# A late u row's fetch is queued two v rows earlier in the dense experts stage

## The reference, cut to what matters

```python
idx = jnp.take_along_axis(cand_i, best_p, axis=-1)       # 128 experts of 16384 for each token
gate = jax.nn.softmax(best_s, axis=-1)
act = jnp.einsum('td,thkd->thk', xb, u_tab[ib])          # x . u of each chosen expert
wgt = jax.nn.gelu(act) * gb
y = jnp.einsum('thk,thkd->td', wgt, v_tab[ib])           # weighted sum of the v rows
```

## Time and profile before

| | us |
|---|---|
| median of three runs | 3286.01 |
| the profiled execution, its own time | 3282.5 |
| its span | 3280.7 |
| PE busy | 3122.7 (95%) |
| DVE busy | 2381.6 (73%) |
| ACT busy | 1406.0 (43%) |
| POOL busy | 641.9 (20%) |

### The profile page before, as it was taken

The page is one execution under the profiler, slowest core; times in us unless marked ns, Lnnn a source line. Parts: engine busy times, 40 slices in busy tenths (PEclk is TensorE's granted clock), DMA queues, the critical chain, the costliest instruction groups (busy, mean ns, idle before and its releaser), DMA issues. The chain is left out here.

```text
span 3280.7 us, 52721 instructions
## 1 busy us (share of the span) xinstructions
PE 3122.7 (95%) x17744; PEld 2695.4 (82%) x17744; DVE 2381.6 (73%) x4997; ACT 1406.0 (43%) x2735; POOL 641.9 (20%) x556
## 2 busy tenths in 40 slices
PE   7899999999999999899989999999999989999999
PEld 5757776777768899888976988988879977988888
DVE  6567776876656686556977777877656788877887
ACT  5454333333346565565264333332564274333332
POOL 0000000000000000155262222222356061222221
PEclk9899999999999999899999999999999999999999
DMA  6115533445323555433518899998334518998996
GB/s 218 42 58 180 173 141 122 141 129 166 95 67 109 159 168 172 142 113 129 176 43 290 316 331 336 334 336 327 129 101 155 167 70 301 338 332 312 338 341 246
DMA packets 176404, 643.35 MB, mean 196 GB/s; under 512 B 20352, under 2 KB 20736, under 8 KB 175360
## 3 DMA queue, kind: packets, MB, share of 16 engines
q1 hardware_dynamic: 138672, 504.62, 45.2%
q0 software_dynamic: 36864, 134.23, 11.4%
q10 hardware_dynamic: 720, 2.71, 0.2%
HBM read 640.44 MB, written 1.05 MB: 196 GB/s over the span
## 5 line engine op out<-in xcount | busy, mean ns | idle before, releaser
L338 ACT ACTIVATE split<-ring 128x512 fp32r<-128x512 f32 (+1 forms) x644 | 397.7, 624 | 699.3 <-PE ps L224 666.7
L224 PE MATMUL ps<-hT,split 128*128 128x512 f32 (+1 forms) x3504 | 630.5, 341 | 6.5 <-DVEq L322 3.5
L224 PEld LDWEIGHTS ps<-hT,split 128*128 128x128 f32 x3504 | 546.1, 191 | 91.1 <-DVE hT L593 9.7
L2696 PE MATMUL ps<-h2F,gates 128*128 128x192 f32 x3200 | 557.5, 328 | 18.1 <-DMA gates<-peer_u 17.9
L2696 PEld LDWEIGHTS ps<-h2F,gates 128*128 128x128 f32 x3200 | 530.9, 191 | 43.9 <-DMA gates<-peer_u 15.2
L347 POOL TENSOR_TENSOR split<-ring,split 128x512 fp32r<-128x512 f32 x184 | 244.6, 1340 | 1529.4 <-ACT split L338 1524.9
L347 DVE TENSOR_TENSOR split<-ring,split 128x512 fp32r<-128x512 f32 (+1 forms) x460 | 307.5, 679 | 283.8 <-ACT split L338 282.9
L2762 ACT ACTIVATE split<-ring 128x512 fp32r<-128x512 f32 x504 | 317.5, 632 | 348.4 <-PE ps L2713 316.2
L2686 POOL DMA_INDIRECT gates<-peer_rows,row_at x256 | 277.0, 1082 | 855.4 <-DVE row_act L2828 471.9
L2821 DVE TENSOR_TENSOR split<-ring,split 128x512 fp32r<-128x512 f32 x504 | 342.7, 691 | 125.5 <-ACT split L2762 125.3
L2755 ACT ACTIVATE gelu<-ps 128x192 f32<-128x192 f32 x200 | 66.2, 331 | 421.3 <-PE ps L2696 421.3
(11 more groups left out here) (389 smaller groups left out, 4753.0 us busy)
## 6 DMA issues: line engine op xcount, KB each, us to landing
ring<-peer_v SPq DMA_DIRECT2D x256, 512.0 KB, 5.6
gates<-peer_u SPq DMA_DIRECT2D x200, 512.0 KB, 6.6
ring<-w_up SPq DMA_DIRECT2D x88, 512.0 KB, 3.7
ring<-w_choose SPq DMA_DIRECT2D x88, 512.0 KB, 3.4
ring<-w_mixing SPq DMA_DIRECT2D x68, 512.0 KB, 3.5
ring<-w_merge SPq DMA_DIRECT2D x64, 512.0 KB, 4.2
ring<-w_down SPq DMA_DIRECT2D x44, 512.0 KB, 3.6
mix_row_ring<-w_mod SPq DMA_DIRECT2D x40, 512.0 KB, 3.7
```

The source lines that it names most:

```text
L224: ins = nc.tensor.matmul(out, lhsT(a), rhs(b), start=first and n == 0, stop=last and n == len(PASSES) - 1)
L338: self.nc.scalar.activation(self.split[:, self.half_slot(s), 0, cols], self.ring[:, self.slot(s), cols], ACT.Copy).then_inc(self.high_read ...
L2696: last = nc.tensor.matmul(k.ps[:, m % 2, 0:DENSE], k.u_ring[:, m % RAW, c * P:(c + 1) * P], k.h2F[:, c, 0:DENSE], start=c == 0, stop=c == ...
```

## The change

u row j - 28 now stands behind v row j, from j = 32 on, and no u row is left for behind the loop. What `fetch_u` waits for, the slots, the number of fetches and all work of the other engines stay as they were.

```diff
                 weights.fetch(sp, j // RAW, j % RAW)
                 if j in first_u:
                     fetch_u(first_u[j])
-                if j - EARLY - 2 >= RAW:
-                    fetch_u(j - EARLY - 2)
-            for q in range(rows - 2, rows):
-                fetch_u(q)
+                if j - EARLY >= RAW:
+                    fetch_u(j - EARLY)
             if ahead:
                 ahead.begin(sp, weights)
```

## The result

The changed kernel took 3266.78 us in the median of 13 runs (3248.15 to 3275.31), the kernel before 3293.03 us in 13 runs (3278.22 to 3310.24). The ratio is 0.9918 with a 95% interval of 0.9896 to 0.9941: 26 us, 0.8% faster. The forecast was 27.1 us less 1, and a time of 3258. The median of before was itself 7 us higher in 13 runs than in the three shown first.

The account below looks back on a forecast made before the run. PE was taken to bound the kernel, losing time only to late u rows: 3282.5 - 27.1 for waits + 1 for transfers = 3256.4 us, or 3259.9 from the median; predicted 3258, with 8 in 10 for 3248 to 3276.

Parts of the forecast that it names:

- What bounds the kernel: Whole kernel: PE, busy 95% of the span, bounds it; in the late part it waits only for u landings.
- What the waits cost in all: Both layers, first to last activate: excess over the clean beat of 12.97 + 14.16 = 27.1 us, all expected to go.
- The 5.8 us of restarts and short waits: Late part: slower restarts after waits and waits too short to list, about 0.36 us for each of 16, expected to go.
- The 3.5 us for activates at the lower clock: Late part: two activates after long waits run partly at the lower clock, some 1.75 us each, expected to go.
- Why u is late: Late u fetches: lead of 7.6 to 7.9 us against landings up to 9.8; an extra dot product delays the issue.
- The new wait in SP's queue: SP, steady part: the wait for u's slot ends before the next v row could be issued, 4 us to spare; cost nothing.
- At the turn: Start of each late part: v row 33 goes out 1.5 us late behind u row 4's wait; cost 0.
- The transfers: DMA in the stage: full pace needs 338 GB/s against 330 before; cost taken as 1 us, bounds 0 and 20.
- The sum: Whole kernel: 3282.5 - 27.1 + 1 = 3256.4 us, or 3259.9 from the median of the runs shown; predicted 3258.
- the DMA rate: Rival, late part: DMA rate is the true bound, landings grow to 17 us and waits return; 3275 to 3286; chance 0.09.
- half a new wait: Rival, late part: DVE, late with the split gates in extra-dot rows, brings back half the excess; about 3270; chance 0.12.
- the held v rows: Rival, SP's queue: its wait for u's slot holds v rows past their 16.9 us lead; 3299 and more; chance 0.03.

Follow-up runs that it names:

- before_again: The kernel before, unchanged, profiled a second time: 3291.62 us in one run, first to last activate 496.94 and 496.77 us in the two layers.
- one_row: Against the kernel before, late u rows queued one v row earlier, half the change's shift: 3273.73 us, ratio 0.9934.
- one_later: Against the kernel before, late u rows queued one v row later: 3552.04 us, ratio 1.0773.
- half_u: The kernel before, its queue order kept, fetching only half the columns (256 KB) of each late u row: 3271.00 us, ratio 0.9899.
- u_first: The kernel before with the two issues of a step swapped, u row j - 30 in front of v row j: 3263.68 us, ratio 0.9923.
- ahead_256: The kernel before with 256 KB more per late row, issued between the v row and the u row: 3355.23 us, ratio 1.0196.
- more_256: The changed kernel with an unused 256 KB transfer more per late row, issued behind u: 3266.49 us, ratio 0.9919 to the kernel before.
- more_320: The changed kernel with an unused 320 KB transfer more per late row, issued behind u: 3262.34 us, ratio 0.9919 to the kernel before.
- v_held: u row j - 24 queued behind v row j, four rows earlier than in the changed kernel: 3420.34 us, ratio 1.0374 to the kernel before.

## Why the prediction was right

- **What bounds the kernel** held: with the u waits gone, PE is busy for every microsecond of the late part, and no other wait took their place. The beat of 4.926 us, read from 11 clean rows, gave 485.35 us for the new late part, 0.06 us below the measured one. Of the earlier trace rows I had read only ACT's waits for the split buffer, at most 0.9 us; its gelu waited up to 5.9 us for PE in the same view. After the change these waits are at most 2.3 us.
- **What the waits cost in all** held, and the way of counting mattered: the waits listed add up to 17.8 us, the distance between first and last activate gave 27.1, and against that profile 27.0 were won. That the two agree to a tenth is partly luck of the profile: before_again, the same kernel, has 11.5 + 11.4 = 22.9 us of excess, with 17.5 us of listed waits. The medians differ by 26.25 us (the interval of the ratio allows 19 to 34), so they can't tell 22.9 from 27.0. The 5.8 us of restarts and short waits are there in both profiles (5.4 in the second) and went with the waits. The 3.5 us for activates at the lower clock are in the first alone: the clock was granted at 0.50 from 2967 to 2970, behind a wait of 2.1 us, but in before_again the activate after a wait of 2.19 us ran at full pace.

```profile
2967.00:2970.00 3.00, 3.00 (x11) 3.00 (x10) 0.00 (x0) 0.01 (x1) 0.22 (x1) 0.50 0.95 314
```
```profile
2840.64 2.84 PE L2696 MATMUL ps<-h2F,gates 128*128 128x192 f32 x16 [2.19 <-DMA gates<-peer_u]
```

- **Why u is late** held in one_row, one_later and half_u, but was incomplete. I told of the extra dot, which makes the issue late, and of the extra gather. I named the v row issued 0.37 us ahead of u nowhere as a cause; u_first and ahead_256 show it to be one large enough that moving it alone removes the waits.
- **The new wait in SP's queue** cost nothing, as worked out; u goes out 0.90 us behind v in the row shown and 1.21 us in the median, where I had written 0.2 to 1, and the next v row 3.7 us after it, where I had counted 4 to spare. The lead was forecast at 17.1 us and is 16.9; the landings are no shorter than before, as written. **At the turn** the lateness is there and hidden: v row 33 follows v row 32 (issued at 1809.08) after 3.9 us in place of 2.3, and no wait results.

```profile
1812.63 0.33 SPq L2659 DMA_DIRECT2D gates<-peer_u  x1
1813.00 0.43 SPq L255 DMA_DIRECT2D ring<-peer_v  x1
```

- **The transfers**: 338 GB/s were forecast, 339 measured. The 1 us set aside for them was not needed: both late parts are the clean ones.
- **The sum**: a gain of 26.1 us was forecast, the medians give 26.25 and the first pair of late parts 27.0. The time was forecast 9 us too low because it started from one profiled execution and three runs, 3282.5 and 3286.0, while 13 runs have 3293.0 for the kernel before.
- Of the **rivals**, the DMA rate fell with more_256 and more_320, half a new wait with the idle time of 0.0, and the held v rows are real but out of reach, as v_held shows.

## What to carry to other kernels

When a stage has a steady beat, take the distance between the same instruction of its first and last row, less the rows times the clean beat: that is what a late transfer costs, and here it was 1.5 and 1.3 times the listed waits in the two profiles of the kernel before. Compare a transfer's landing with its lead before thinking about rates; a row of lead, half the bytes, or a place ahead of the less urgent transfer in the same queue each removed all of the loss or all but 1.6 us of it, the last without any more depth. When a fetch is moved up, look at what stands behind its wait: up to the point where its slot is free it cost nothing here, beyond it only the neighbour was held back.

## What the runs showed of the hardware that had not been expected

- 256 KB more per row delayed a u row little when issued behind it (8 and 1 us a layer) and much when issued ahead of it (35 us a layer), though the bytes in each row are the same.
- The core took in 406 GB/s for 420 us with PE never idle, 20% more than the changed kernel asks for. But between 395 and 406 GB/s the median landing of a 512 KB row rose from 6.7 to 9.9 us, so only a lead like the changed kernel's 16.9 us hides it.
- What lies outside the changed part differs by 13 us between two profiles of the same kernel (2282.9 and 2296.1), with a granted clock of 0.89 and 0.73 in the first 60 us, and by 30 us over all thirteen.
